# Pass ends, one norm read from PSUM and the last products of an encoder block on one core: reordered queues and spread work

## The reference

```
x += 1/2 * (1+g0) * SwiGLU_1(mod0(RMSNorm(x)))            # D_FF = 2816
h  = mod1(RMSNorm(x)); P = h W_in = [q|k|v|x_c|B|C]
     A: chunked attention, 8 heads, own chunk of 64 + 8 before
     B: B * causal_dwconv3(C * x_c)
x += (1+g1) * W_out [RMSNorm(A) | RMSNorm(B)]
x += 1/2 * (1+g2) * SwiGLU_2(mod2(RMSNorm(x)))
x  = RMSNorm(x) * g_final
```

## Time and profile before

| | before |
|---|---|
| median of three runs, us | 1856.34 |
| profiled execution, us | 1854.08 |
| its span, us | 1852.3 |
| PE busy, share of the span | 96% |
| DVE, ACT, POOL busy | 62%, 36%, 27% |
| granted TensorE clock, mean | 0.989 |

### The profile page before, as it was taken

One profiled execution on the slowest core, in us unless ns is written; L12 is line 12 of the kernel. 1 busy time (PEld: TensorE's weight loads), 2 busy tenths in 40 slices (PEclk: granted clock), 3 DMA queues, 4 the chain that ended last, 5 costly groups with the idle time before them and its releaser, 6 DMA issues.

```text
span 1852.3 us, 21181 instructions
## 1 busy us (share of the span) xinstructions
PE 1780.2 (96%) x8256; PEld 1465.1 (79%) x8256; DVE 1148.8 (62%) x1346; ACT 669.3 (36%) x859; POOL 495.4 (27%) x279
## 2 busy tenths in 40 slices
PE   3989999999999989999999999999999999999997
PEld 2778888888788778877788788788888888888875
DVE  7978777666787572446554467676444444568756
ACT  3443323333343442325333144334333333333342
POOL 1146555654100000204212031215344543310000
PEclk9999999999999999998999999999999999999998
DMA  9035664456867324331232320402332233585633
GB/s 364 23 121 189 206 211 170 164 195 219 306 228 244 91 63 125 91 108 46 74 131 91 97 75 1 160 0 97 108 129 93 93 100 98 194 298 207 229 89 107
DMA packets 84658, 260.96 MB, mean 141 GB/s; under 512 B 8160, under 2 KB 8160, under 8 KB 83040
## 3 DMA queue, kind: packets, MB, share of 16 engines
q1 hardware_dynamic: 79968, 251.49, 40.0%
q10 hardware_dynamic: 4608, 8.39, 1.2%
HBM read 211.09 MB, written 48.76 MB: 140 GB/s over the span
## 4 chain that ended last, share of the span: by engine, by line
PE 83%; issue 6%; DVE 6%; ACT 2%; DMA 1%; POOL 1%; SPq 1%; POOLq 0%; DVEq 0%; ACTq 0%
PE pair L2090 20%; PE pair L2092 20%; PE pair L2091 20%; PE pair L2084 6%; PE pair L2086 6%; PE pair L2085 6%; PE pair L2424 2%; PE pair L2390 1%; PE pair L2405 1%; DVE ada L1476 1%; DVE w_lo L1394 1%; DMA raw<-hs 1%; DVE cb L1537 1%; DMA x<-xT 0%; DVE x L1503 0%
## 5 line engine op out<-in xcount | busy, mean ns | idle before, releaser
L2090 PE MATMUL pair<-cb,w_hi 128*128 128x512 f32 x864 | 338.1, 391 | 8.8 <-DVE w_lo L1394 5.8
L2091 PE MATMUL pair<-cb,w_hi 128*128 128x512 f32 x864 | 337.6, 391 | 0.0
L2092 PE MATMUL pair<-cb,w_lo 128*128 128x512 f32 x864 | 337.4, 391 | 0.0
L2090 PE MATMUL pair<-h_hi,w_hi 128*128 128x512 f32 x824 | 322.4, 391 | 11.8 <-DVE w_lo L1394 9.2
L2092 PE MATMUL pair<-h_hi,w_lo 128*128 128x512 f32 x824 | 321.8, 391 | 0.0
L2091 PE MATMUL pair<-h_lo,w_hi 128*128 128x512 f32 x824 | 321.6, 390 | 0.0
L2090 PEld LDWEIGHTS pair<-cb,w_hi 128*128 128x128 f32 x864 | 163.2, 189 | 43.7 <-DVE w_lo L1394 6.6
L2090 PEld LDWEIGHTS pair<-h_hi,w_hi 128*128 128x128 f32 x824 | 155.5, 189 | 45.2 <-DVE w_lo L1394 9.6
L2092 PEld LDWEIGHTS pair<-cb,w_lo 128*128 128x128 f32 x864 | 163.0, 189 | 34.2
L2091 PEld LDWEIGHTS pair<-cb,w_hi 128*128 128x128 f32 x864 | 163.1, 189 | 33.9
L2091 PEld LDWEIGHTS pair<-h_lo,w_hi 128*128 128x128 f32 x824 | 155.5, 189 | 32.3
(11 more groups left out here) (182 smaller groups left out, 3203.6 us busy)
## 6 DMA issues: line engine op xcount, KB each, us to landing
raw<-hs SPq DMA_DIRECT2D x70, 512.0 KB, 3.9
ada_w<-w_ada SPq DMA_DIRECT2D x55, 512.0 KB, 4.2
raw<-w_mix SPq DMA_DIRECT2D x48, 512.0 KB, 3.5
hs<-tt SPq DMA_DIRECT2D x20, 1024.0 KB, 6.4
a<-w_f1o SPq DMA_DIRECT2D x30, 512.0 KB, 6.7
a<-w_f2o SPq DMA_DIRECT2D x30, 512.0 KB, 5.7
ga<-w_f1i SPq DMA_DIRECT2D x22, 512.0 KB, 4.4
ua<-w_f1i SPq DMA_DIRECT2D x22, 512.0 KB, 4.4
```

Of the source, the lines that this page charges most:

```text
L2090: nc.tensor.matmul(dst, lh, rh, start=first, stop=False, skip_group_check=True)
L2091: nc.tensor.matmul(dst, lh, rl, start=False, stop=False, skip_group_check=True)
L2092: return nc.tensor.matmul(dst, ll, rh, start=False, stop=False, skip_group_check=True)
```

## The change

Six edits, in the order of the kernel:

1. **SP, end of each SwiGLU's groups:** the loads of the hidden chunks 2, 3 and 4 and `hid_last` move ahead of part of the a21 and a22 weights.
2. **Modulation:** the block before `down(0)` is split over iterations 2, 21, 22 and 23 of `down(0)`.
3. **Down products:** the four `x_update` of step 4 go ahead of the splitting of chunk 32; chunk 41 is split in iteration 37 along with chunk 40; in `down(0)` `h_first` alternates between `tmp` and `qsq`, and `h_second` comes one tile later; at the end the first two updates, the first mixer weights and the sums of squares take another order.
4. **First half's convolution norm:** no `spread`; `conv_first` reads 1/rms from the PSUM bank and waits for `bc_done`.
5. **SwiGLU 2, first group:** `norm_stats(7)` goes behind the second block of products, `norm_spread(7)` into the third, after two of its four k.
6. **End:** `last_stats` adds the last square on PE in place of DVE's addition. 1/rms is spread into two banks. DVE reads one in six of the eight last products; ACT copies the other for POOL, which makes tiles 6 and 7 (ACT has multiplied them by g_final during step 6).

```diff
@@ sync, end of ffn_loads
-                for c in range(OC):
+                for c in range(3):
                     down_load(F, 1, a21, c, a21_in)
                 hid_load(F, 2)
+                for c in range(3, OC):
+                    down_load(F, 1, a21, c, a21_in)
+                hid_load(F, 3)
+                hid_last(F)
+                sp.wait_ge(hs_out, stored(F, g - 1))
                 sp.wait_ge(w_used, n + 5)
-                for c in range(OC - 1):
+                for c in range(2):
                     down_load(F, 3, a22, c, a22_in)
-                hid_load(F, 3)
-                sp.wait_ge(hs_out, stored(F, g - 1))
                 hid_load(F, 4)
-                hid_last(F)
+                for c in range(2, OC - 1):
+                    down_load(F, 3, a22, c, a22_in)
@@ gpsimd, behind power(9)
+            pool.wait_ge(rstd_done, rstd_count(9))
+            for i, k in enumerate(FINAL_POOL):
+                pool.wait_ge(xg_done, i + 1)
+                nc.gpsimd.tensor_tensor(col(out_sb1, k * T, T), xt(1, k), col(rstd, T, T), ALU.mult).then_inc(out_rest, 1)
@@ scalar, down
-                    if q + 3 < OQ:
+                    if q + 3 < OQ - 1:
                         out_hi(F, q + 3)
                         hid_hi(F, q + 3)
+                    if q + 4 == OQ - 1:
+                        out_hi(F, q + 4)
+                        hid_hi(F, q + 4)
...
+                        if F == 1 and KH + c in FINAL_POOL:
+                            k = KH + c
+                            nc.scalar.activation(xt(1, k), xt(1, k), ACT.Identity,
+                                                 scale=sm[:, SM_GF + k:SM_GF + k + 1]).then_inc(xg_done, 1)
...
                 for e in range(KH):
-                    if F == 0 and e == 3:
-                        mix_hi(MX[0])
-                        mix_hi(MX[0] + 1)
+                    if F == 0 and e < 2:
+                        mix_hi(MX[0] + e)
@@ scalar, mixer
-                    if s == CONV_SPREAD[mx]:
+                    if mx == 1 and s == CONV_SPREAD[mx]:
                         spread(NORM_CONV[mx], col(rstd, mx * T, T))
@@ scalar, end
-            spread(9, col(rstd, T, T))
-            for m in range(KD, HALVES * KD):
-                store(m)
+            act.wait_ge(bc_again, 1)
+            nc.scalar.copy(col(rstd, T, T), bank[SPREAD_BANK][:]).then_inc(rstd_done, 1)
+            for m in range(3):
+                store(KD + m)
+            store_rest(0)
+            store(KD + 3)
+            store(KD + 4)
+            store_rest(1)
+            store(KD + 5)
@@ vector, down (out_lo and hid_lo change as out_hi and hid_hi)
+                    if c == OC - 1 and s == 4:
+                        for e in range(KH):
+                            x_update(F, s, e)
...
+                    if F == 0:
+                        modulation_rest(q)
...
                             h_first(1, k, 1, 0)
-                            h_second(1, k, 1)
+                            if k:
+                                h_second(1, k - 1, 1)
...
-                for e in range(KH):
-                    if F == 0 and e == 3:
-                        mix_lo(MX[0])
-                        mix_lo(MX[0] + 1)
-                    x_update(F, STEPS - 1, e)
-                    add_square(n1, KH + e)
                 if F == 0:
+                    h_second(1, KD - 1, 1)
+                    x_update(0, s, 0)
+                    x_update(0, s, 1)
+                    mix_lo(MX[0])
+                    add_square(n1, KH)
+                    mix_lo(MX[0] + 1)
...
@@ vector, conv_first
+                    if ct == 0 and mx == 0:
+                        dve.wait_ge(bc_done, NORM_CONV[0] + 1)
...
+                    r = col(rstd, T, T) if mx else bank[STAT_BANK[NORM_CONV[0]]][:]
                     nc.vector.scalar_tensor_tensor(tmp[:], col(yc, ct * T, T), sm[:, SM_GC + ct:SM_GC + ct + 1],
-                                                   col(rstd, mx * T, T), ALU.mult, ALU.mult).then_inc(y_tmp, 1)
+                                                   r, ALU.mult, ALU.mult).then_inc(y_tmp, 1)
@@ tensor, first_group_mixed
                 pe.wait_ge(x_done, CREDIT + KD + 4)
                 plain(1, 0, "B11", GATE0, True)
+                plain(1, 1, "B21", GATE0, False).then_inc(first_mm, 1)
                 pe.wait_ge(x_done, CREDIT + 2 * KD)
                 norm_stats(7)
-                plain(1, 1, "B21", GATE0, False).then_inc(first_mm, 1)
-                norm_spread(7)
-                plain(1, 2, "B11", UP0, True)
+                plain(1, 2, "B11", UP0, True, between=lambda: norm_spread(7))
```

More of the change, by code:

```diff
@@ L333, in build @@
         out_stored = sem("out_stored")
+        xg_done = sem("xg_done")
+        out_rest = sem("out_rest")
+        bc_again = sem("bc_again")
         block = ctx.enter_context(nc.Block())
@@ L412, in gate, with h_buf, rstd_count @@
             return mod[:, f:f + 1]
+        FINAL_POOL = (6, 7)
+        SPREAD_BANK = 7
+        def h_buf(inst, m):
+            return qsq if inst == 1 and m % 2 else tmp
+        def rstd_count(n):
+            return n + 1 - (n >= NORM_CONV[0])
         def in_chunk(F, g, c):
@@ L1717, in final, with modulation_rest @@
                                                col(rstd, hf * T, T), ALU.mult, ALU.mult).then_inc(out_done, 1)
+            def modulation_rest(q):
+                if q == 2:
+                    dve.wait_ge(ada_done, ADA_TILES)
+                    modulation(0, (2,))
+                if q == 21:
+                    modulation(1, (0, 1))
+                if q == 22:
+                    modulation(1, (2,))
+                    modulation(2, (0, 1))
+                if q == 23:
+                    modulation(2, (2,))
+                    shift_step(1)
             def down(F):
@@ L1739, in down @@
                         if k == 0:
[L1740 removed]
+                            dve.wait_ge(rstd_done, rstd_count(n0))
                         if F == 0:
                             h_first(1, k, 1, 0)
[L1743 removed]
+                            if k:
+                                h_second(1, k - 1, 1)
                         else:
                             final(k, 0, out_sb)
[L1746 removed]
+                    if c == OC - 1 and s not in (4, STEPS - 1):
                         for e in range(KH):
                             x_update(F, s, e)
[L1749 to L1755 removed]
+                s = STEPS - 1
+                if F == 0:
+                    h_second(1, KD - 1, 1)
[4 more added lines that the diff above has]
+                    mix_lo(MX[0] + 1)
+                    add_square(n1, KH + 1)
+                    x_update(0, s, 2)
+                    add_square(n1, KH + 2)
+                    x_update(0, s, 3)
+                    add_square(n1, KH + 3)
                     mix_lo(MX[0] + 2)
                     mix_lo(MX[0] + 3)
+                else:
+                    for e in range(KH):
+                        x_update(1, s, e)
+                        if e < KH - 1:
+                            add_square(n1, KH + e)
             dve.wait_ge(small_in, 16)
@@ L2115, in norm_stats, with last_stats @@
                 mm.then_inc(stat_mm, 1)
+            def last_stats(n):
+                pe.wait_ge(acc_done, norm_acc(n) + NORM_TILES[n])
+                for t in range(TT):
+                    nc.tensor.matmul(bank[STAT_BANK[n]][:, t:t + 1], acc[:, t * P:(t + 1) * P], one2[:, 0:1],
+                                     start=t == 0, stop=False, skip_group_check=True)
+                pe.wait_ge(sq_done, norm_sq(n) + NORM_TILES[n])
+                for t in range(TT):
+                    mm = nc.tensor.matmul(bank[STAT_BANK[n]][:, t:t + 1], sq[:, t * P:(t + 1) * P], one2[:, 0:1],
+                                          start=False, stop=True, skip_group_check=True)
+                mm.then_inc(stat_mm, 1)
             def norm_spread(n):
@@ L2143, in in_mm, with plain @@
                             k == 0 and kind in ("A11", "S1", "A12"))
-            def plain(F, c, block, to, first, rest=False):
+            def plain(F, c, block, to, first, rest=False, between=None):
                 slot = in_slot(F, c)
@@ L2164, in plain @@
                         mm = more(bank[2 * to[F] + j][:], *w_block(slot, KH * j + k), rh, rl, first and k == 0)
+                    if between is not None and k == 1:
+                        between()
                 return mm
@@ L2521, in _ @@
                         mixer(mx)
-            norm_stats(9)
+            last_stats(9)
             norm_spread(9)
+            for t in range(TT):
+                r = rinv[:, t:t + 1]
+                src = bass.AP(r.tensor, r.offset, [list(r.ap[0]), [0, P]])
+                mm = nc.tensor.transpose(bank[SPREAD_BANK][:, t * P:(t + 1) * P], src, ident[:])
+            mm.then_inc(bc_again, 1)
 def kernel(**inputs):
```

47 lines of the change are left out of this document (27 added, 20 removed).

## The result

The kernel after takes 1834.42 us, the median of four runs between 1834.02 and 1834.64; the kernel before takes 1856.2 on the same chip (four runs, 1855.88 to 1856.45). The ratio is 0.9883, with a 95% interval of 0.987 to 0.9895, so 21.8 us went. The forecast was 1831.8 with a range of 1828 to 1841: 2.6 us too low, and inside. The profiled execution of after takes 1834.46, its span is 1832.7 (before: 1852.3).

The account below looks back on a forecast made before the run. PE, busy 96% of the span, bounds the kernel, so only its pauses, low clock and tail count. Terms sum to 24.5 us: 1854.1 gives 1829.6, plus 2.3 for the median 1831.8; range 1828 to 1841.

Parts of the forecast that it names:

- Start of down(0): PE's wait for hidden chunk 3's low half goes, with DVE's modulation block moved and loads earlier: 2.3 us.
- Steps 4 to 5: Down products, both passes: x updates ahead of chunk 32's splitting remove both PE pauses, 3.5 us.
- chunk 41: Down products, both passes: split one iteration earlier, PE's waits for its low half go, 3.1 us.
- Entry to the mixer: First mixer weights ready about 1.2 us before PE; the pause and low clock behind it go: 4.5 us.
- Rival B: Down product's end: ACT late with first mixer weights, clock falls again; nothing of 4.5 left, 1836.3 us; chance 0.13.
- Convolution norm: mixer(0): multiplies no longer held by POOL; 2.85 us of pauses and three fifths of clock time, 6.0 us.
- Rival A: Clock in mixer(0) stays low, only the holds go: 2.5 in place of 6.0, giving 1835.3 us; chance 0.20.
- SwiGLU 2, first group: Ready products ahead remove PE's wait for POOL's sum and the low clock after it: 4.4 us, floor 2.0.
- Rival C: SwiGLU 2's group 1 waits for ACT's gz instead, 2.4 us, giving 1834.2 us; chance 0.10.
- End: DVE's last addition and its wait for ACT's copy leave the chain: 0.65 us, bounds 0 and 1.4.
- the first store goes out there: Kernel's end: ACT's copy stays in place, ending near 1844.3; the first store issues then, not at 1845.04.
- Rivals D and E: Edits don't do what they say, 1854 to 1858, chance 0.03; slower through late a22 loads, e.g. 1862, chance 0.02.

Follow-up runs that it names:

- after_old_loads: The kernel after with SP's old load order back (hidden chunks 2 to 4 and last hidden activations behind the same weights as before); 1834.29 us, one run.
- before_with_psum_norm: The kernel before with only the first half's convolution norm changed to read 1/rms from PSUM; 1853.37 us, ratio to before 1.0001.

## Why the prediction was right, and where not

- **Start of down(0)**, 2.3 forecast, 2.35 found. The steps hold: chunk 3's low half is ready at 483.4 in after. With the late load and no block I had it ready at 488.3; in after_old_loads it was 489.2, since DVE split it late and in 1.70 us, and that was still in time. The two moved groups of work cost nothing.
- **Steps 4 to 5**, 3.5 against 3.7; **chunk 41**, 3.1 against 3.4. The 0.16 us that a pause costs beyond its idle time is borne out: at the products right behind them the pauses of 1.62 (in both passes) and 2.37 gave 1.78 and 2.54. The ledger's 1.91 and 2.77 hold small differences between the places besides.
- **Entry to the mixer**, 4.5 against 4.4. No pause over 0.2 us, clock 1.00. Rival B didn't come.
- **Convolution norm**, 6.0 against about 0.9 in the ledger: the step that failed. Two terms of it did. Of the pauses I took 2.85; PE's pauses in the attention of mixer(0) went from 3.8 to 2.5 us, 1.3 less, since of the 3.3 for nmax 1.2 stayed and ytok came in with 0.8, a wait that before has not in this half. Of the clock I took three fifths of 5.1 us, reading the low clock of before as the consequence of its pauses; it came without them, and the 10 us at 0.50 cost 5.0 again. That is the sign that I had named, a clock below 0.8 in the scores. Rival A had the outcome, a clock that stays low when only the holds go; it also counted the holds at 2.5 in place of 1.3, and why the clock falls is open. With the clock held up by filling, the same edit gave 4.6 in one pair of traces.
- **SwiGLU 2, first group**, 4.4 against 4.4, with gz's pause going from 0.45 to 0.74. Rival C came as that third of a microsecond, not as 2.4.
- **End**, 0.65 against 1.3. The step that failed is "the first store goes out there", at the end of ACT's copy. The trace shows the store issued at 1825.43, 0.01 us behind the copy's start at 1825.42 and not behind its end: 5.87 us behind the x update, 7.15 before. The 0.58 us of the copy should not have stood in the sum.
- **mixer(1)**, 0 against -0.6: in the profiled run a wait for ACT's s_sb went from 0.56 to 1.15. It was 0.59 with the block of modulation, 0.71 to 0.96 in others and 0.72 in the second trace of after itself, so it moves from run to run; its cause is open.
- **Rivals D and E**: nothing of either. SP is in order, the a22 weights behind hid_load(4) stop no one.

The terms' sum was 24.5, the ledger's 19.6. The misses of -5.1 (norm), -0.4 (start), -0.6 (mixer(1)) and +0.65 (end), +0.6 (the others), make -4.9. The median missed by only 2.6 because the profiled execution of before, to whose time I had added 2.3 us for the median, lay 2.3 us below its median, and that of after did not. That 2.3 was a property of one run and not of the kernel; I took it for an offset that both have, and by luck it went against the error.

## What to carry to other kernels

Before a pause is priced with the low clock behind it, look whether the clock falls in the same loop where there is no pause; if it does, the pause's removal gives back only the pause, or nothing, until the loop is made denser, and a few useless wide products may do that: here ten of them, 2.3 us of work, saved a stretch that cost 5. Where two delays stand in series ahead of a need with little room, undo each alone and both together before one is called the cause. And hold effects of a microsecond against the starts of the same instruction in two traces, not against medians that a varying clock spreads over several.

## What the runs showed of the hardware

- The granted clock fell to 0.50 for 10 us behind 10 us in which PE was busy for 9.24, with no pause over 0.54 us; by times and mean clocks this came in eight of nine runs of one and the same kernel. The Trainium skill, TensorE: Matmul & The Clock Gate, in its table Why this matters for your kernels, ties such a fall to long pauses between bursts of products; the longest pause in mixer(0) is 0.78 us in after and 2.2 in any trace here. With ten or twenty products of 512 columns among the thin ones the clock was 1.00 there in both traces that also had the new norm, and the mean clock was 0.993 or 0.994 in all eight runs.
- The reverse also: a pause of 2.64 us at the mixer's entry in before_with_psum_norm was followed by clock 1.00, one of 2.62 at the same place in before by 0.61.
- In both traces of after a DMA issue behind a copy on ACT's queue begins 0.01 us behind the copy's start; its data don't come from that copy.
- A multiply with one operand in PSUM takes 0.74 to 0.75 us, the same as with both in SBUF and POOL at rest. The 0.065 us more for each that I had estimated from the Trainium skill's page VectorE: DVE Perf Modes is not to be seen.
- The last 2.1 MB take 7.2 to 7.3 us from the first store's issue to the end, with 377 to 385 GB/s in the five full microseconds in the middle, whether two products come from POOL or none.
